# The second FFN emits the out-projection: tiles in its own order, products by output half

## The reference, cut to what matters

```python
def _swiglu(x, w_gate, w_up, w_down):
    return (jax.nn.silu(x @ w_gate) * (x @ w_up)) @ w_down
...
    x = _layernorm(ALPHA * x + 0.5 * _swiglu(x, lp['ffa_w_gate'], lp['ffa_w_up'], lp['ffa_w_down']), lp['ln1_g'], lp['ln1_b'])
    m, ckv, kr, wkv, buf = _token_mixer(x, pos, shift_buf, wkv0, attend, **mp)     # ends: concatenate([y_mla, y_rw]) @ w_out
    x = _layernorm(ALPHA * x + m, lp['ln2_g'], lp['ln2_b'])
    x = _layernorm(ALPHA * x + 0.5 * _swiglu(x, lp['ffb_w_gate'], lp['ffb_w_up'], lp['ffb_w_down']), lp['ln3_g'], lp['ln3_b'])
```

## Time and profile before

| | |
|---|---|
| median of 3 runs | 2453.66 us (2445.74 to 2467.68) |
| profiled execution | 2459.68 us, span 2458.0 us |
| PE busy, share of the span | 2371.1 us, 96% |
| DVE, ACT, POOL busy | 1567.6, 1012.3, 432.8 us |
| PE busy from 1619.5 to 1715.5 (out-projection) | 95.92 of 96.00 us |
| PE busy from 1715.5 to 1747.0 (to the FFN's first matmul) | 16.75 of 31.50 us |

### The profile page before, as it was taken

How to read it: one execution, slowest core, us unless ns; L and a number is a source line. 1 busy time by engine, 2 the same in 40 slices (tenths; PEclk the granted TensorE clock), 3 DMA queues, 4 the chain that set the end, 5 groups by cost and what they waited for, 6 DMA issues and landing times.

```text
span 2458.0 us, 52723 instructions
## 1 busy us (share of the span) xinstructions
PE 2371.1 (96%) x21093; PEld 2101.3 (85%) x21093; DVE 1567.6 (64%) x2730; ACT 1012.3 (41%) x1786; POOL 432.8 (18%) x421
## 2 busy tenths in 40 slices
PE   8999999999999999999999999999799999999997
PEld 7999999988878799666657988877799999998886
DVE  6777766565685847677633444463777776666568
ACT  5333333354545646433333333342533333345343
POOL 4232100000042212000000122333522210000005
PEclk8999999999999999999999999999899999999999
DMA  4465523397554444422122022244355552339653
GB/s 159 163 204 173 199 82 113 113 316 231 177 186 134 136 114 118 134 58 61 33 70 101 28 73 66 72 164 138 128 197 195 175 187 83 110 129 316 214 174 116
DMA packets 306657, 346.59 MB, mean 141 GB/s; under 512 B 39633, under 2 KB 206370, under 8 KB 304882
## 3 DMA queue, kind: packets, MB, share of 16 engines
q1 hardware_dynamic: 252946, 286.85, 36.2%
q10 hardware_dynamic: 52256, 53.62, 6.2%
q0 software_dynamic: 1216, 2.80, 0.4%
HBM read 244.25 MB, written 98.41 MB: 139 GB/s over the span
## 4 chain that ended last, share of the span: by engine, by line
PE 83%; DVE 8%; issue 4%; ACT 3%; POOL 1%; DMA 1%; SPq 0%; ACTq 0%; POOLq 0%; DVEq 0%
PE ps_b L763 18%; PE ps_a L763 17%; PE ps_a L473 6%; PE ps_b L473 6%; PE ps_rk L3077 6%; PE ps_pj L1525 4%; PE ps_wo L3872 4%; PE ps_mp L2265 3%; PE ps_mp L2291 2%; PE ps_pj L1507 2%; PE ps_mp L2279 1%; PE ps_rk L3167 1%; PE ps_mp L2250 1%; DVE W_a L1061 1%; PE ps_rk L3073 1%
## 5 line engine op out<-in xcount | busy, mean ns | idle before, releaser
L763 PE MATMUL ps_b<-X_b,W_b 128*128 128x272 f32 x3696 | 466.3, 289 | 4.5 <-DVE X_b L1022 3.9
L763 PEld LDWEIGHTS ps_b<-X_b,W_b 128*128 128x128 f32 x3696 | 464.9, 189 | 5.9 <-DVE X_b L1022 4.1
L763 PE MATMUL ps_a<-X_a,W_a 128*128 128x272 f32 x3696 | 465.4, 288 | 4.5 <-DVE X_a L1022 1.7
L763 PEld LDWEIGHTS ps_a<-X_a,W_a 128*128 128x128 f32 x3696 | 463.5, 189 | 6.4 <-DVE G_a L1079 3.0
L473 PE MATMUL ps_a<-W_a,H_a 128*128 128x512 f32 x924 | 216.1, 390 | 0.0
L473 PE MATMUL ps_b<-W_b,H_b 128*128 128x512 f32 x924 | 214.8, 389 | 1.0 <-DVE H_b L1108 1.0
L473 PEld LDWEIGHTS ps_b<-W_b,H_b 128*128 128x128 f32 x924 | 173.3, 188 | 37.3 <-DVE W_b L1061 1.4
L473 PEld LDWEIGHTS ps_a<-W_a,H_a 128*128 128x128 f32 x924 | 173.8, 188 | 36.0
L844 ACT ACTIVATE W_a<-wraw_a 128x512 fp32r<-128x512 f32 x154 | 95.8, 629 | 163.7 <-PE ps_a L763 65.1
L844 ACT ACTIVATE W_b<-wraw_b 128x512 fp32r<-128x512 f32 x154 | 95.8, 629 | 162.7 <-PE ps_b L763 64.4
L1061 DVE TENSOR_TENSOR W_b<-wraw_b,W_b 128x512 fp32r<-128x512 f32 x154 | 113.7, 744 | 69.4 <-ACT W_b L844 69.4
(11 more groups left out here) (495 smaller groups left out, 4290.7 us busy)
## 6 DMA issues: line engine op xcount, KB each, us to landing
hraw_a<-hidden SPq DMA_DIRECT2D x77, 256.0 KB, 3.6
hraw_b<-hidden SPq DMA_DIRECT2D x77, 256.0 KB, 3.7
wraw_pj<-in_w_in SPq DMA_DIRECT2D x28, 512.0 KB, 3.7
wraw_a<-in_ffa_w_gate SPq DMA_DIRECT2D x22, 512.0 KB, 4.7
wraw_a<-in_ffa_w_up SPq DMA_DIRECT2D x22, 512.0 KB, 4.9
hraw_a<-in_ffa_w_down SPq DMA_DIRECT2D x22, 512.0 KB, 5.4
down_sums<-hraw_a SPq DMA_DIRECT2D x11, 1024.0 KB, 6.5
wraw_a<-down_sums SPq DMA_DIRECT2D x44, 256.0 KB, 2.9
```

What stands on the lines that cost most here:

```text
L763: last = nc.tensor.matmul(ps[:, bank + p, :PIECE], W[:, n % WC, wp, k * P:(k + 1) * P], operand(i, xp)[:, k, p * PIECE:(p + 1) * PIECE], s ...
```

## The change

The second FFN runs the out-projection's parts itself (`before.sync`, `before.tensor`, `before.scalar`, `before.vector`, `before.pool`), in each engine's program ahead of its own, so that steps of the two can be mixed:

- the row tiles of the out-projection go in `X_ORDER`; n is the position in it
- the product of a tile is made by output half: all 24 matmuls of columns 0 to 511, then those of 512 to 1023; residual and statistics follow by half (`RowNorm.half`). Only banks 0, 1 (n = 0), 6, 7 (output) and 4, 5 (transposes of y) are used, so banks 0 to 3 are free for items 1 to 3 of the FFN
- SP, for n = 2 to 7, waits for the store of row n - 2 and loads it for the FFN; PE transposes it between the two halves of tile n
- ACT, DVE and POOL prepare item j = 0 and j = 1 between steps of the out-projection (ACT ahead of `y_high` 5 and 7, DVE between the half sums of n = 3 and 5, POOL ahead of `right` 3 and 5); the third item follows the last tile's statistics, mixed with its norm; the other two follow
- the states' store goes ahead of the weight loads 5 to 7, and DVE waits for it to land between the low parts 3 and 4; the gains are loaded behind the last split of the weights
- the operand of both FFNs is cut into 256 and 288 columns (`LEFT`, `RIGHT`) instead of 272 and 272; the buffers of out-projection and FFN lie differently in SBUF, and the down-projection's first slots wait for other up slots
- the out-projection has semaphores of its own (`LnSems`)

```diff
-HALF, PIECE = 544, 272
+HALF, LEFT, RIGHT = 544, 256, 288
...
+    def half(self, dve, chain, n, c):
+        if c == 0:
+            dve.wait_ge(N.res_in[s].h, N.res_in[s].at(16 * (n // 2 + 1)))
+            if n >= ZS:
+                dve.wait_ge(N.stored[n % ZS].h, N.stored[n % ZS].at(16 * (n // ZS)))
+            if n >= 2:
+                dve.wait_ge(N.scaled.h, N.scaled.at(n - 1))
+        self.half_sum(dve, n, c, z[:, cols], x[:, cols]).then_inc(N.z_made.h, 1)
...
@@ ffn, SP
             if before is not None:
-                before.store(sp, NT - 2)
+                before.sync(sp, load_x)
+                load_w(0)
+                load_x(6)
+                load_x(7)
+                before.weights_read(sp)
+                load_w(1)
+                before.last_row(sp)
+                load_x(8)
...
@@ ffn, up_slot
-                            last = nc.tensor.matmul(ps[:, bank + p, :PIECE], W[:, n % WC, wp, k * P:(k + 1) * P],
-                                                    operand(i, xp)[:, k, p * PIECE:(p + 1) * PIECE],
+                            last = nc.tensor.matmul(ps[:, bank, 512 - LEFT:] if p == 0 else ps[:, bank + 1, :RIGHT],
+                                                    W[:, n % WC, wp, k * P:(k + 1) * P], operand(i, xp, p)[:, k, :],
...
@@ ffn, PE
+            if before is not None:
+                before.tensor(pe, turn)
+                before.banks_free(pe)
+            for k in range(0 if before is None else 6, NT):
                 turn(k)
...
@@ out_projection, SP
+            before.store_states(sp)
+            before.products(sp)
             for k in range(WS, KD):
                 load_w(k)
...
+            for n in range(NT):
+                norm.load_rows(sp, n)
+                if n == 0:
+                    sp.wait_ge(R["w_split"].h, R["w_split"].at(KD))
+                    norm.load_gains(sp)
+                if n >= 2:
+                    norm.store(sp, n - 2)
+                if n + 2 < NT:
+                    rows_in(n + 2)
...
+                if 2 <= n < NT - 1:
+                    load_x(n - 2)
+            norm.store(sp, NT - 2)
...
@@ out_projection, PE
+            for n in range(NT):
+                r, s = rows_of(tiles[n]), n % 2
+                pe.wait_ge(R["ylo"].h, R["ylo"].at(n + 1))
+                if 3 <= n < NT - 1:
+                    turn(n + 1)
...
+                for c in range(2):
+                    if n >= 2:
+                        pe.wait_ge(N.z_made.h, N.z_made.at(2 * (n - 1) + c + 1))
+                    for k in range(KD):
+                        if n == 0 and c == 0:
+                            pe.wait_ge(R["w_split"].h, R["w_split"].at(k + 1))
+                        for m, (a, b) in enumerate(((yhi, w_high_at), (yhi, w_low_at), (ylo, w_high_at))):
+                            last = nc.tensor.matmul(ps[:r, out_bank(n) + c, :], a[:, s, k, :r], b(k)[:, c * 512:(c + 1) * 512],
+                                                    start=(k == 0 and m == 0), stop=(k == KD - 1 and m == 2))
+                        if c == 0 and k == 3 and n < 3:
+                            turn(n + 1)
+                    last.then_inc(R["m_done"].h, 1)
+                    if c == 0 and 2 <= n < NT - 1:
+                        turn_x(n - 2)
...
@@ out_projection, ACT
+        def item(self, act, j):
+            if j == 0:
+                act.wait_ge(R["w_split"].h, R["w_split"].at(KD))
+                before.rows_landed(act)
+            if j == 2:
+                act.wait_ge(R["m_done"].h, R["m_done"].at(2 * NT))
+                norm.wait_stored(act, NT - 2)
+                norm.wait_stored(act, NT - 3)
+            if j == 3:
+                act.wait_ge(N.z_made.h, N.z_made.at(2 * NT))
...
+            for n in range(2, NT):
+                if n in (5, 7):
+                    x_parts(n // 2 - 2)
+                y_high(n)
+                norm_rows(n - 2)
+            norm_rows(NT - 2)
+            x_parts(2, lambda: norm.root(act, NT - 1), lambda: norm.scale(act, NT - 1))
...
@@ out_projection, DVE
+            for k in range(2, 4):
+                w_low(k)
+            before.states_landed(dve)
+            for k in range(4, 6):
                 w_low(k)
             before.norm_dve(dve, chain, NGR - 2)
             for k in range(6, KD):
                 w_low(k)
...
+            for n in range(NT):
+                norm.half(dve, chain, n, 0)
+                if n in (3, 5):
+                    x_parts(n // 2 - 1)
+                norm.half(dve, chain, n, 1)
+                norm.variance(dve, n)
+                if n >= 1:
+                    norm.gain(dve, n - 1)
+                if n < NT - 1:
+                    norm.inverse(dve, chain, n)
+                if n + 2 < NT:
+                    y_low(n + 2)
+            x_parts(2, lambda: norm.inverse(dve, chain, NT - 1), lambda: norm.gain(dve, NT - 1))
...
@@ out_projection, POOL
+            for n in range(NT - 1):
+                if n in (3, 5):
+                    sums_low(n // 2 - 1, range(4))
+                norm.right(pool, chain, n)
+            sums_low(2, range(2))
+            norm.right(pool, chain, NT - 1)
+            sums_low(2, range(2, 4))
```

More of the change, by code:

```diff
@@ L825, in _ @@
             pe.wait_ge(S.const_ready.h, S.const_ready.at(1))
-            for k in range(NT):
-                if before is not None and k in (0, 2):
-                    before.free(pe, k // 2)
+            if before is not None:
+                before.tensor(pe, turn)
+                before.banks_free(pe)
+            for k in range(0 if before is None else 6, NT):
                 turn(k)
@@ L939, in scale_res @@
                 nc.scalar.activation(z_of(t), z_of(t), ACT.Copy, scale=2 * ALPHA).then_inc(Q.res_scaled.h, 1)
-            for j in range(5):
+            if before is not None:
+                before.scalar(act, x_parts)
+            for j in range(0 if before is None else 3, 5):
                 if j == 4:
@@ L1125, in token_sum @@
                 V.tensor_tensor(z, z, ps[:TS, bank, :], ALU.add).then_inc(Q.z_made.h, 1)
-            for j in range(5):
+            if before is not None:
+                before.vector(dve, chain, x_parts)
+            for j in range(0 if before is None else 3, 5):
                 if j == 4:
@@ L3744, in rwkv, with out_projection @@
     return End()
-def out_projection(nc, S, blk, sems, before, y_mla, y_rw, w_out, x_src, g_dram, b_dram, dst):
-    tiles = list(range(NT))
+def out_projection(nc, S, sems, before, y_mla, y_rw, w_out, x_src, g_dram, b_dram, dst):
+    tiles = X_ORDER
     wdr = w_out.rearrange("(k p) c -> p k c", p=P)
@@ new lines, in out_projection, with raw, w_high_at, w_low_at @@
+    w_in = [Sem(nc, sems, f"wo_w_in{u}") for u in range(WS)]
+    y_in = [Sem(nc, sems, f"wo_y_in{u}") for u in range(2)]
+    N = LnSems(nc, sems)
+    def raw(k):
+        return wraw[:, k % WS * D:(k % WS + 1) * D]
+    def w_high_at(k):
+        return whi[:, k, :]
+    def w_low_at(k):
+        return wlo[1][:, (k + 1) % 3, :] if k < 3 else wlo[0][:, k - 3, :]
+    def out_bank(n):
+        return 0 if n == 0 else 6
+    def half_sum(dve, n, c, z, x):
+        dve.wait_ge(R["m_done"].h, R["m_done"].at(2 * n + c + 1))
+        if n == 0:
+            before.values_read(dve, NGR - 2 + c)
+        return nc.vector.scalar_tensor_tensor(z, x, ALPHA, ps[:rows_of(tiles[n]), out_bank(n) + c, :], ALU.mult, ALU.add)
```

508 lines of the change are left out of this document (231 added, 277 removed).

## The result

The changed kernel takes 2508.11 us, the median of 4 runs (2504.75 to 2513.88). The kernel before, run beside it, took 2450.53 (2445.74 to 2467.68). The ratio is 1.0225, 95% interval 1.0170 to 1.0279: slower by 2.2%, between 1.7 and 2.8. The forecast was 2500, range 2474 to 2522.

What follows compares the result with a forecast made beforehand. The out-projection was taken as bound by PE at 12.1 us a tile, the seam by VectorE and ScalarE. 31 + 10 + 8 - 2.5 = +46.5 us on the 2453.7 median gave 2500 us, range 2474 to 2522.

Steps and rivals of the forecast that it cites:

- Part 1, rows late: Tiles 2 to 7: PE waits 4.3 us for each row's store and load; +31 us (28 to 42), added transposes included.
- Part 2, clock: Tiles 2 to 7: each PE wait halves the clock for 3.4 us; +10 us (0 to 20).
- Part 3, head: Out-projection's head: late weights, then a second half wholly behind the last weight, delay tile 1; +8 us (4 to 10).
- "Other SBUF places" at nothing: Remaining edits, such as moved SBUF buffers and own semaphores, change only waits met long before; costed at nothing.
- Part 4, seam: Out-projection's last matmul to the second FFN's first: 29 us against 31.5; -2.5 us (-7 to +2).
- The second branch: In the seam, the last tile's gain, add, store, load and transposes reach E + 24.3 (E: last matmul's end), then filling transposes.
- Part 5, pieces: Both FFNs' matmuls cut into 256 and 288 columns go by columns; change 0, other end +24 us.
- the second (clock holds): Rival: rows late in the tiles, but the clock holds in waits and the head costs 6; 2488 us, chance 0.17.
- the third: Rival: slower row loads in the tiles, 2511 us, or slower 256-column matmuls in the FFNs, 2524; chance together 0.14.
- the held piece: Rival case in both FFNs: 256-column matmuls held at 125.5 ns, +24 us, 2524 us; chance 0.14 shared with slower row loads.
- the longer loads (4.9 us): Rival case in the tiles: row loads behind y loads, +1.8 us six times, 2511 us; chance 0.14 shared with slower 256-column matmuls.
- The other side (rows in time, 2460 or 2448): Tiles without PE waits for rows: 2460 us, chance 0.12; with a free head and both items out of the seam 2448, 0.05.

Runs made afterwards that it cites:

- own gain: Changed kernel with VectorE doing each tile's gain at the end of its own iteration, not behind the next tile's statistics: 2464.44 us, ratio 1.0044.
- the late row: Changed kernel with row n-3, not n-2, transposed in tile n and item preparation one iteration later: 2467.20 us, ratio 1.0049.
- the filled wait: Changed kernel with 42 transposes of the identity on PE ahead of the transposes of x: 2499.33 us, ratio 1.0171.

## Why the prediction was right, point by point

- **What bounds the kernel:** right. PE had no slack in the tiles, so each of its waits is paid in full: 32.7 us of waits are 32.7 us of the stretch.
- **Part 1, rows late:** the mechanism was right in each step. S + 4.8 for the add and S + 7.7 for the store were forecast and measured. The load's landing was mis-sized: 3.1 us forecast, 4.09 in the tile shown and 3.8 in the median. The y rows ahead of it are part of the reason; issued ahead of them it still took 3.6. At full clock a tile became 18.4 us instead of 17.3, so the rows cost (18.4 - 12.1) x 6 = 38 us, not 31, inside the bounds of 28 to 42. That nothing catches up was right: six tiles of 19.5 to 21.0 us. The stall ends once the gain, or the row's turn, moves by one step (the runs with own gain and with the late row).
- **Part 2, clock:** right as a mechanism, and in size by some luck. 1.8 us a tile instead of 1.7, 10.5 instead of 10, by the filled wait. But the half clock lasted 6.8 us a tile (3.4 in the first), not 3.4, and it cost so little only because PE was idle for part of it: busy 3.88 of 6.80 in the stretch shown.
- **Part 3, head:** the sum was nearly right (9.5 against 8), its first part too: late weights cost 5.4 us alone, the clock's 1.8 included. The second part, the rest of the 8 us, for a second half wholly behind the last weight, isn't shown to cost anything. 78 matmuls behind the split of weight 6 instead of 60 (12 of tile 0 and 48 of tile 1 in the kernel before) are there in the trace, but taking them away gave 0.4 us, as another wait stands right behind. It is the one I costed at nothing. So the size is in part luck. The clock's loss, named there without a number, is some 2.3 us.
- **"Other SBUF places" at nothing:** in the changed kernel right, as a size; as a reason wrong. The wait of tile 0's second half sum for GpSimd is 6.9 us long and not met long before. It was covered by the late PE, and showed as 5.4 us (18.1 instead of 12.7 in one tile) once the rows were in time.
- **Part 4, seam:** right in place and order, -1.3 us instead of -2.5. The second branch set it: last add, store, load, transposes, the 28 filling ones. The last load took 3.5 us instead of 2.7.
- **Part 5, pieces:** 0, by the groups of matmuls in the profile after and by the run of its own. The forecast's 5.5 ns for 16 columns isn't the slope of the clock, as it says; 16 columns at 2.4 GHz are 6.7.
- **The rivals:** the second (clock holds) is refuted by the clock row of 0.50 and by the filled wait. Of the third, the held piece is refuted, and the longer loads (4.9 us) were half met: 3.8 in the median, between the forecast's 3.1 and its 4.9. The other side (rows in time, 2460 or 2448) was built by experiment: 2454.2, between its two values, with the head at 9.8 and 10.8 back from the seam.
- **The sum:** 46.5 forecast on the median. By stages it was 55.1. The difference of 8.6 is +7 for the rows, +1.5 for the head, +0.5 for the clock, +1.2 for the seam and -1.6 for the rest, which is what the two executions differ by in unchanged work. Between the medians the change was 57.6 us, 11 more than forecast; 2508 came instead of 2500, and not 2511, since the kernel before was at 2450.5 in this comparison and not at the 2453.7 that I added to. That part of the nearness is luck.

## What to carry to other kernels

When work is moved under a stage that one engine fills, ask at what time its input is ready there, step by step from the event that starts the loop, over the store and the load if it goes over HBM: here 11.8 us against 6.5 available, paid six times and once more by the clock. Look at where the last step of the producer stands in its engine's program before moving anything: one instruction of 0.57 us placed one tile earlier took away five of six stalls. And a wait that costs nothing because a worse one covers it has to be written down, since it is the next one when the worse one is mended; the same holds for a transfer, where taking away a wait left four transfers of 512 KB under way at once and the load took 6.5 us instead of 4.1.

## What the runs showed of the hardware

- A store of 512 KB landed in 2.6 us with nothing issued behind it, and in 2.9 with 512 KB of y rows issued behind it within 0.9 us. A load of 512 KB took 3.4 to 6.7 us with 2 MB issued within some 3 us. Ahead of the y rows its median was 3.6 us instead of 3.8; issued 1.3 us earlier, ahead of the store's landing, it took 2.4 longer in the tile shown, and 5.1 in the median.
- 512-column fp32r matmuls were 227 ns apart in the order by output half, and 233 in the order that changes the half at each matmul (24 in 5.46 us against 5.61, 48 in 11.21). Why isn't known: the runs changed bank order and half together. It gave 0.3 us a tile back, so that the 8 added transposes of 0.87 us cost 0.6.
- Idle waits of some 5 us in every tile brought 6.8 us at half clock each (3.4 behind the first), and transposes of the identity in the wait kept the clock at 1.00. A wait that was 0.8 us shorter gave nothing, as more work fell under the half clock (5.35 us instead of 3.88).
